# One layer of a hybrid decoder on one core: prompt attention moved between the products of the value stage

## The chip, the cores and the metric

The kernel runs on one NeuronCore of one Trainium2 chip. The metric is the device time of one execution in microseconds (us): the median over the timed runs. In the names below, PE is the matrix engine (TensorE), DVE the vector engine, ACT the scalar engine, POOL the general engine (GpSimd), which here also issues DMAs, and SP the queue that issues the weight loads.

## The reference, cut to what matters

One trunk layer handles a prompt of 272 tokens (16 meta tokens and 256 of the sequence) and 64 decode tokens (8 sequences of 8) with the same weights. What the change touches is the attention of the prompt and the state of the convolution:

```python
q = rmsnorm(q.reshape(B, T, N_HEADS, HEAD_DIM), q_g)      # 8 heads of 128
k = rmsnorm(k.reshape(B, T, N_HEADS, HEAD_DIM), k_g)
v = v.reshape(B, T, N_HEADS, HEAD_DIM)
...
s = index_scores(iqb, iwb, ik, qp, k_pos)                  # an indexer picks 64 keys per query
_, sel = lax.top_k(s, top_k)
logits = einsum('bqhd,bqkhd->bhqk', q, k_sel) * HEAD_DIM ** -0.5 + bias(rel)
p = softmax(logits); o = einsum('bhqk,bqkhd->bqhd', p, v_sel)
...
full = concatenate([ctx, u], axis=1)                       # 30 old rows of each sequence, then the new ones
```

The normed keys and the values of all tokens are outputs too (`k_prompt`, `v_prompt`, `k_sample`, `v_sample`), by token. The decode tokens attend to 64 pages of 128 cached keys; that work follows the prompt's attention.

## The kernel before, in words

All projections run with the output channels on the partitions and the 336 tokens as columns. A weight block of 2048 x 128 (one *unit*) is loaded to one of four slots of `RAW`; ACT rounds it to `WH`, DVE writes the rest to `WL`, four *quarters* each, two units ahead of PE; PE then multiplies it in 48 products (`split_mm`: `WH` with `XH`, `WH` with `XL`, `WL` with `XH`), 12 to a quarter, into one of two accumulators `psG`. The order of the work is written out by hand for each engine, and semaphores join the engines; nothing is scheduled. Each engine takes its own list strictly in order, PE too: a product that stands behind a wait waits with it.

Stages that matter here, in program order:

- **qk**: 16 units make queries and keys; DVE norms each (`nm_done` counts them) and takes the best scores of the indexer out in rounds of eight (`take8`). At its end DVE turns the scores of the prompt into a mask `Wp` (`p_mask`, before line 1060).
- **v**: 8 units, one for each head. ACT copies each accumulator to `vT`; PE turns it to token order (`v_by_token`, four turns), one unit later; DVE copies the turned tiles to `vtok`, `v2`, `vs` (`vk_done`).
- **prompt**: after the last value unit, 16 tiles (2 query tiles of 128 for 8 heads; the first sees 144 keys, the second 272). For tile i: PE makes logits (`p_logits`: query by key, and the mask added through the identity), DVE scales, adds the bias `Tb` and takes the maximum, ACT does the exponential (`p_soft`), DVE divides (`p_norm`), PE turns the weights (`p_turn`), ACT copies them to `pT`, PE multiplies them with the values (`p_values`), DVE copies the result to `oT`. The tiles go query tile by query tile, through four logit banks.
- **key turns**: 24 turns of the keys to token order through two banks; ACT copies them to `ktok`, which has two slots of two heads; heads 4 to 7 wait until the stores of heads 0 to 3 have landed (`ko_wr`). Then 128 small products give the logits of the decode tokens among themselves (`ln_mm`).
- **state turns**: 16 turns of the old convolution rows (`sct`), copied to `ub`.
- **cz**: 16 units of the convolution's input; between quarters PE turns one cached key page (8 turns) and after every second page multiplies it. POOL loads the pages into four slots of `kst`; it issues the first page after the last state turn has been copied (`sc_cp`), and page n + 4 when page n has been turned (`k_tr`).

Of the kernel before, what the change touches and what calls it, by code (L numbers as in the profile page):

```python
# [27 lines left out]
ALU = mybir.AluOpType  # L28
# [98 lines left out]
def place(persistent, transient):  # L127
# [42 lines left out]
    ("ub", [P, CT, UW], F32, ST_KOUT, ST_NORM),  # L170
    ("oT", [P, H, NQ], F32, ST_PROMPT, ST_WA),
# [31 lines left out]
    ("v2", [16, CC], F32, ST_V, ST_KOUT), ("Tb", [P, H, NP], F32, ST_V, ST_PROMPT),  # L203
    ("sct", [120, 2, CC], F32, ST_KOUT, ST_KOUT),
    ("Lp", [P, 4, NP], F32, ST_PROMPT, ST_PROMPT), ("pT", [P, 2, 3, P], F32, ST_PROMPT, ST_PROMPT),
    ("ktok", [P, 2, 3, 2 * P], F32, ST_KOUT, ST_KOUT), ("qsz", [P, H, B, 32], F32, ST_V, ST_CZ),

    ("kst", [P, 4, CC], F32, ST_CZ, ST_CZ), ("kTs", [P, 2, H, P], F32, ST_CZ, ST_CZ),
# [13 lines left out]
PLACING = ("Ss Ws SGA ub oT vs m8s cmp gsb QK qsz IW Sp Wp esel qm cms ikTa hT ML SGB L ikst oh iqT vtok iqs v2 iktok relb "  # L222
           "bT7 bNw relx vst CH CL Tb ikb osb wrow yp ya PTn ikT iwT rf cblk m8p xtok xs xTs kst OH csq rl sct kTs ktok "
           "ytok pairM Lp utok ustok pT sq rt vT sq2 gt at rp sel uss sgt crt sqa ut prow rln iwtok e8 ").split()


def layer(nc, I, O):
# [62 lines left out]
    with ExitStack() as ctx:  # L290
# [109 lines left out]
        def _(pool):  # L400
# [41 lines left out]

            pool.wait_ge(nm_done, 2 + 2 * H)
# [3 lines left out]
            pool.wait_ge(g_wr, 16)  # L447
            pool.dma_start(Tb[:], bass.AP(tensor=gscr, offset=P - 1, ap=[[RELW - 1, P], [P * RELW, H], [1, NP]])).then_inc(tb_ld, 16)
            pool.dma_start(O["conv_sample"][0, :, 0:CTX - Q], I["state_conv"][0, :, Q:CTX]).then_inc(cs_wr, 16)
            pool.wait_ge(vk_done, 2 + H)  # L450
            vp = O["v_prompt"][0, 0].rearrange("t h d -> t (h d)")
            pool.dma_start(vp[0:2 * P].rearrange("(i p) n -> p i n", p=P), vtok[:]).then_inc(v_wr, 16)
            pool.dma_start(vp[2 * P:NP], v2[:]).then_inc(v_wr, 16)
            pool.dma_start(O["v_sample"][0].rearrange("b q h d -> (b q) (h d)"), vs[:]).then_inc(v_wr, 16)
            pool.wait_ge(p_o, 2 * H)
            for i in range(2):
                pool.dma_start(sct[:, i, :], I["state_conv"][0, 4 * i:4 * i + 4].rearrange("b w c -> (b w) c")).then_inc(side_ld, 16)
            pool.memset(ub[:, :, 0:UPAD], 0.0).then_inc(ub_z, 1)
# [3 lines left out]
            for h in range(1, H, 2):  # L462
# [6 lines left out]
            pool.wait_ge(v_wr, 48)  # L469
            for i in range(4):  # L470
                pool.wait_ge(ko_wr[i], (16 if i < 2 else 32) * H // 4)
            pool.wait_ge(qs_dn, 1)
            pool.wait_ge(p_o, 2 * H)
            pool.wait_ge(sc_cp, CT)
# [9 lines left out]

            pool.sem_inc(k_tr, 4)
            k_pages = pages(kst, cache_k, k_ld, k_tr)
            k_pages(0)
            pool.dma_start(cblk[:], I["c_blk"]).then_inc(side_ld, 16)
# [44 lines left out]
        def _(act):  # L533
# [140 lines left out]
            def v(g):  # L674
                for s in range(4):
                    ahead(G0["v"] + g, s)
                    done(G0["v"] + g, s)
                    act.wait_ge(nm_done, 2 + 2 * H)
                    act.activation(vT[:, s % 2, :], G[s % 2][:, 0:NT], ACT.Copy).then_inc(ev[s % 2], 1)

            loop(act, GN["v"], v)

            act.wait_ge(qz, 1)
# [4 lines left out]
            def p_soft(i):  # L688
                nk = keys_of(i // H)
# [4 lines left out]
            p_soft(0)  # L694
            p_soft(1)
            for i in range(2 * H):
                if i + 2 < 2 * H:
                    p_soft(i + 2)
# [3 lines left out]
                full = i // H + 1  # L702
                act.activation(pT[:, i % 2, 0:full, :], MB[i % 2][:, 0:full * P].rearrange("p (k n) -> p k n", k=full), ACT.Copy)
                act.activation(pT[0:N_META, i % 2, full, :], MB[i % 2][0:N_META, full * P:full * P + P], ACT.Copy).then_inc(p_cp, 1)
            act.wait_ge(p_o, 2 * H)
            kp = O["k_prompt"][0, 0].rearrange("t h d -> t (h d)")
            for h in range(H):
# [5 lines left out]
                act.activation(ktok[:, slot, 0:2, c], TB[h % 2][:, 0:2 * P].rearrange("p (i d) -> p i d", i=2), ACT.Copy)  # L713
                act.activation(ktok[0:NT - 2 * P, slot, 2, c], TB[h % 2][0:NT - 2 * P, 2 * P:3 * P], ACT.Copy).then_inc(ko_cp, 1)
# [3 lines left out]
            for c in range(CT):  # L718
                act.wait_ge(sc_tr, c + 1)
                act.activation(ub[:, c, UP:UW].rearrange("p (b w) -> p b w", b=B)[:, :, 0:CTX],  # L720
                               MB[c % 2][:, 0:B * CTX].rearrange("p (b w) -> p b w", b=B), ACT.Copy).then_inc(sc_cp, 1)

# [3 lines left out]
            def cz(g):  # L726
                for s in range(4):
                    for j in range(4):
                        act.wait_ge(k_tr, g * 16 + (4 * s + j + 5))
                        act.activation(kTs[:, j % 2, 0:4, :], TB[0][:].rearrange("p (h n) -> p h n", h=4), ACT.Copy).then_inc(kc_A, 1)  # L730
                        ahead_quarter(G0["cz"] + g, s, j)
                    if s % 2 == 0:
                        done(G0["cz"] + g, s)
                        act.wait_ge(ev[1], 2 * (G0["cz"] + g) + (1 + s // 2))
                        act.activation(sgt[:], G[0][:, 0:NT], ACT.Sigmoid).then_inc(ev[0], 1)

            loop(act, GN["cz"], cz)
# [159 lines left out]
        def _(dve):  # L897
# [168 lines left out]
            def v(g):  # L1066
                def copy(s):
                    c = bass.ds(g * 4 * P + P * s, P)
                    dve.wait_ge(vtr, g * 4 + (s + 1))
                    dve.tensor_copy(vtok[:, :, c], MB[s % 2][:, 0:2 * P].rearrange("p (i d) -> p i d", i=2))  # L1070
                    dve.tensor_copy(v2[:, c], MB[s % 2][0:N_META, 2 * P:3 * P])
                    dve.tensor_copy(vs[:, c], MB[s % 2][0:NS, 3 * P:4 * P]).then_inc(vk_done, 1)

                ch.loop(g, 8)
                for s in range(4):
                    ahead(G0["v"] + g, s)
                    take8(m8s[:], Ws[:])
                    if s:
                        copy(s - 1)
                copy(3)  # L1080

            loop(dve, GN["v"], v)
            ch.end(GN["v"])


            sbank = [SB[0], SB[1], TB[0], TB[1]]

            def p_logits(i):
                qt, h = i // H, i % H
# [7 lines left out]
                dve.scalar_tensor_tensor(row, sbank[i % 4][:, 0:nk], SC, Tb[:, h, z0:z0 + nk], ALU.mult, ALU.add).then_inc(p_lg, 1)  # L1097
# [3 lines left out]
            def p_norm(i):  # L1101
                nk = keys_of(i // H)
# [5 lines left out]
            def p_out(i):  # L1108
                qt, h = i // H, i % H
# [3 lines left out]
            p_logits(0)  # L1113
            p_logits(1)
            for i in range(2 * H):
                if i + 2 < 2 * H:
                    p_logits(i + 2)
                if i >= 2:
                    p_out(i - 2)
                p_norm(i)  # L1120
# [4 lines left out]
            dve.wait_ge(ub_z, 1)  # L1125

            def cz(g):
                ch.loop(g, 8)
                for s in range(4):
# [13 lines left out]
                    done(G_, s)  # L1143
                    dve.tensor_tensor(ub[:, c, UPAD:UP], G[1][:, None, 0:NP], sgt[:, None, 0:NP], ALU.mult)
# [775 lines left out]
```

## Time and profile before

| | |
|---|---|
| median of 3 runs | 2144.13 us (2141.44 to 2153.07) |
| the profiled execution's own time | 2145.37 us |
| its span, first to last instruction | 2143.9 us |
| PE busy | 2064.7 us (96%) |
| DVE busy | 1247.2 us (58%) |
| ACT busy | 901.2 us (42%) |
| POOL busy | 165.7 us (8%) |
| mean granted clock of TensorE | 0.97 |

The page gives each engine's busy time over the whole span, and slices of it. The stretch that the change touches runs from 323.00 us, the first product of the value stage, to 457.37 us, the first turn of a cached key page. Rows of a timeline give the start in us, the time in us, the engine, the line, the operation and its operands, the count, and in brackets the idle time before it and what ended that. Weight products show a time longer than their pitch, since they are pipelined; a product of two fp32 operands shows as two records.

### The profile page before, as it was taken

The numbers are of one execution on the slowest core, as the hardware profiler recorded it, in microseconds if no ns is written. First come the engines' busy times: TensorE is split into PE (matmuls) and PEld (weight loads), VectorE is DVE, ScalarE is ACT, GpSimd is POOL, SyncE is SP. The second block draws the span as 40 slices with busy tenths as digits, with TensorE's granted clock in tenths as the row PEclk, the third lists the DMA queues.
The fourth block names the chain that finished last, engine by engine and source line by source line (L and its number), as shares of the span: only waits on it lengthen the run. The fifth ranks groups of instructions, "written<-read, shape, count | busy, mean of one in ns | idle before, by whom it ended". The sixth has DMA issues, their size and how long they took to land.

```text
span 2143.9 us, 40449 instructions
## 1 busy us (share of the span) xinstructions
PE 2064.7 (96%) x14517; PEld 1958.8 (91%) x14517; DVE 1247.2 (58%) x2293; ACT 901.2 (42%) x1647; POOL 165.7 (8%) x293
## 2 busy tenths in 40 slices
PE   6989999879998999999999999999999999999997
PEld 5956999769996777999999999999999999999997
DVE  5324988626666899875665545554455554445553
ACT  5423443434444333436444544543344443344443
POOL 6300000021112121001000000000000000000012
PEclk8997999879998999999999999999999999999999
DMA  8352456257776898455655555555555555555573
GB/s 232 93 113 40 122 133 172 66 163 237 239 240 197 267 327 271 133 143 155 191 156 148 146 156 139 155 147 147 157 143 151 153 142 156 149 145 157 144 207 110
DMA packets 545492, 350.54 MB, mean 164 GB/s; under 512 B 15122, under 2 KB 524346, under 8 KB 545007
## 3 DMA queue, kind: packets, MB, share of 16 engines
q1 hardware_dynamic: 518480, 263.55, 45.7%
q0 software_dynamic: 25824, 84.55, 12.4%
q8 instruction: 69, 1.13, 0.2%
q10 hardware_dynamic: 1088, 1.05, 0.1%
q14 instruction: 31, 0.25, 0.0%
HBM read 338.91 MB, written 10.83 MB: 163 GB/s over the span
## 4 chain that ended last, share of the span: by engine, by line
PE 67%; DVE 1%; ACT 0%; issue 0%; POOL 0%; POOLq 0%; DVEq 0%; ACTq 0%
PE psG L1380 21%; PE psG L1381 21%; PE psG L1382 20%; PE psS L1377 2%; PE psM L1380 1%; PE psM L1382 1%; PE psM L1381 1%; PE psM L1374 0%; PE psG L1374 0%; DVE stat L1186 0%; DVE OL L1249 0%; ACT L L752 0%; PE psT L1374 0%; DVE L L1181 0%; DVE L L1182 0%
## 5 line engine op out<-in xcount | busy, mean ns | idle before, releaser
L916 DVE TENSOR_TENSOR WL<-RAW,WH 128x512 fp32r<-128x512 f32 (+1 forms) x996 | 673.2, 691 | 642.9 <-ACT WH L551 641.3
L551 ACT ACTIVATE WH<-RAW 128x512 fp32r<-128x512 f32 (+1 forms) x996 | 615.7, 628 | 850.8 <-PE psG L1382 806.1
L1380 PE MATMUL psG<-XH,WH 128*128 128x320 f32 (+1 forms) x2688 | 854.5, 318 | 8.3 <-ACT iwT L629 5.3
L1381 PE MATMUL psG<-XL,WH 128*128 128x320 f32 (+1 forms) x2688 | 843.3, 314 | 0.0
L1382 PE MATMUL psG<-XH,WL 128*128 128x320 f32 (+1 forms) x2688 | 841.4, 313 | 0.0
L1380 PEld LDWEIGHTS psG<-XH,WH 128*128 128x128 f32 x2688 | 511.5, 190 | 40.1 <-issue 31.3
L1381 PEld LDWEIGHTS psG<-XL,WH 128*128 128x128 f32 x2688 | 511.8, 190 | 1.1
L1382 PEld LDWEIGHTS psG<-XH,WL 128*128 128x128 f32 x2688 | 511.8, 190 | 0.0
L1380 PE MATMUL psG<-MH,WH 128*128 128x320 f32 x960 | 297.9, 310 | 0.3 <-DVE ML L1349 0.3
L1382 PE MATMUL psG<-MH,WL 128*128 128x320 f32 x960 | 296.6, 309 | 0.0
L1381 PE MATMUL psG<-ML,WH 128*128 128x320 f32 x960 | 296.6, 309 | 0.0
L1380 PEld LDWEIGHTS psG<-MH,WH 128*128 128x128 f32 x960 | 180.5, 188 | 0.5 <-issue 0.5
L1381 PEld LDWEIGHTS psG<-ML,WH 128*128 128x128 f32 x960 | 180.5, 188 | 0.0
L1382 PEld LDWEIGHTS psG<-MH,WL 128*128 128x128 f32 x960 | 180.5, 188 | 0.0
L1213 DVE SCALAR_TENSOR_TENSOR ya<-ub,wdw,ya 128x256 f32<-128x256 f32 x232 | 99.8, 477 | 0.0
L522 POOL DMA_DIRECT2D out<-ytok x16 | 11.6, 726 | 1083.6 <-ACT ytok L876 1079.6
L1374 PE MATMUL psT<-ident,kst 128*128 128x128 f32 x512 | 68.9, 278 | 5.9 <-DMA kst<-in_cache_k 5.9
L1374 PEld LDWEIGHTS psT<-ident,kst 128*128 128x128 f32 x512 | 58.2, 142 | 12.8 <-issue 12.3
L1134 DVE COPY kTs<-psT 128x512 f32<-128x512 f32 x64 | 43.9, 686 | 42.8 <-PE psT L1374 42.8
L730 ACT ACTIVATE kTs<-psT 128x512 f32<-128x512 f32 x64 | 38.3, 598 | 46.5 <-PE psT L1374 46.2
L866 ACT ACTIVATE MH<-at 128x320 f32 x44 | 20.8, 472 | 82.9 <-DVE at L1347 82.9
L482 POOL DMA_DIRECT2D kst<-in_cache_k x64 | 33.8, 528 | 176.2 <-issue 176.2
(354 smaller groups left out, 1704.2 us busy)
## 6 DMA issues: line engine op xcount, KB each, us to landing
RAW<-in_w_in SPq DMA_DIRECT2D x160, 512.0 KB, 5.3
RAW<-in_w_ffn_down SPq DMA_DIRECT2D x96, 512.0 KB, 4.8
RAW<-in_w_ffn_gate SPq DMA_DIRECT2D x88, 512.0 KB, 4.9
RAW<-in_w_ffn_up SPq DMA_DIRECT2D x88, 512.0 KB, 4.6
kst<-in_cache_k POOLq DMA_DIRECT2D x64, 512.0 KB, 4.5
vst<-in_cache_v POOLq DMA_DIRECT2D x64, 512.0 KB, 5.9
RAW<-in_w_out SPq DMA_DIRECT2D x32, 512.0 KB, 4.8
RAW<-in_w_attn_br SPq DMA_DIRECT2D x16, 512.0 KB, 4.9
```

Of the source, the lines that this page charges most:

```text
L482: pool.dma_start(dst[:, n:n + 1, :], src[bass.ds(page(g * m + n, ptab2), 1)].rearrange("o s n -> s o n")).then_inc(landed[n], 16)
L551: act.activation(WH[:, s % 2, 4 * r:4 * r + 4, c], RAW[:, s, 4 * r:4 * r + 4, c], ACT.Copy).then_inc(hi_done, 1)
L730: act.activation(kTs[:, j % 2, 0:4, :], TB[0][:].rearrange("p (h n) -> p h n", h=4), ACT.Copy).then_inc(kc_A, 1)
L866: act.activation(MH[:, bass.ds(g * 2 + s // 2, 1), :], at2[:, s // 2:s // 2 + 1, :], ACT.Copy).then_inc(ah_dn, 1)
L916: dve.tensor_tensor(WL[:, s, k, c], RAW[:, s, k, c], WH[:, s % 2, k, c].bitcast(F32), ALU.subtract).then_inc(lo_done, 1)
L1134: dve.tensor_copy(kTs[:, j % 2, 4:8, :], TB[1][:].rearrange("p (h n) -> p h n", h=4)).then_inc(kc_D, 1)
L1213: ch.step(dve.scalar_tensor_tensor(z, x, tap, z, ALU.mult, ALU.add))
L1374: return pe.transpose(out, src, ident[0:n, 0:n])
L1377: return pe.matmul(out, lhsT, rhs, start=start, stop=stop, skip_group_check=True)
L1380: pe.matmul(out, WH[:, s % 2, k], hi, start=start, stop=False)
L1381: pe.matmul(out, WH[:, s % 2, k], lo, start=False, stop=False)
L1382: return pe.matmul(out, WL[:, s, k], hi, start=False, stop=stop)
```

## The change

The 16 tiles of the prompt's attention are now taken head by head (tile i is head i // 2, query tile i % 2) and placed behind the quarters of the value units: unit u carries the logits of head u, and the turns, the value products and the turns of the keys of head u - 1. The last head's rest follows behind the last unit. The value turns use bank `psT0`, the key turns bank `psT1`, the logits one bank for each query tile. The 16 state turns go to the first group of the cz stage, one pair behind each of its last eight quarters. POOL issues the bias table `Tb` earlier, and the first four key pages right after the last value copy (`vk_done`), ahead of the stores of the values; it waits for those stores, for the key stores and for `ln_mm` before it clears the padding of `ub` and goes on with page 4. Placement in SBUF (`PLACING` and the stages of some tiles) is changed to suit. The diff, cut to its core:

```diff
@@ POOL
+            pool.wait_ge(pp_acc, 2 * IH)
+            pool.wait_ge(d_ss, 1)
+            pool.wait_ge(g_wr, 16)
+            pool.dma_start(Tb[:], ...).then_inc(tb_ld, 16)
             pool.wait_ge(nm_done, 2 + 2 * H)
             pool.wait_ge(o_ik, 48)
             pool.memset(qsz[:], 0.0).then_inc(qz, 1)
...
-            pool.wait_ge(sc_cp, CT)
...
+            pool.wait_ge(vk_done, 2 + H)
             pool.sem_inc(k_tr, 4)
             k_pages = pages(kst, cache_k, k_ld, k_tr)
             k_pages(0)
+            pool.dma_start(vp[0:2 * P].rearrange("(i p) n -> p i n", p=P), vtok[:]).then_inc(v_wr, 16)
+            pool.dma_start(vp[2 * P:NP], v2[:]).then_inc(v_wr, 16)
+            pool.dma_start(O["v_sample"][0]..., vs[:]).then_inc(v_wr, 16)
+            keys_out(H - 1)
+            pool.wait_ge(p_o, 2 * H)
+            for i in range(2):
+                pool.dma_start(sct[:, i, :], ...).then_inc(side_ld, 16)
+            pool.wait_ge(qs_dn, 1)
+            pool.wait_ge(ln_mm, 1)
+            pool.wait_ge(v_wr, 48)
+            for i in range(4):
+                pool.wait_ge(ko_wr[i], (16 if i < 2 else 32) * H // 4)
+            pool.memset(ub[:, :, 0:UPAD], 0.0).then_inc(ub_z, 1)
             pool.dma_start(cblk[:], I["c_blk"]).then_inc(side_ld, 16)
             with pool.Fori(1, B * NPG // 4) as g:
                 k_pages(g)
@@ ACT
+            act.wait_ge(nm_done, 2 + 2 * H)
+            for u in range(H):
+                G_, s = G0["v"] + u // 4, u % 4
+                if u:
+                    v_kept(u - 1)
+                ahead_quarter(G_, s, 0)
+                if u:
+                    p_turned(2 * u - 2)
+                ahead_quarter(G_, s, 1)
+                if u:
+                    p_turned(2 * u - 1)
+                p_soft(2 * u)
+                ahead_quarter(G_, s, 2)
+                p_soft(2 * u + 1)
+                ahead_quarter(G_, s, 3)
+                if u:
+                    key_by_token(u - 1)
@@ DVE
+            for u in range(H):
+                G_, s = G0["v"] + u // 4, u % 4
+                if u:
+                    v_by_token(u - 1)
+                ahead_quarter(G_, s, 0)
+                best8(m8s[:], Ws[:])
+                p_logits(2 * u)
+                ahead_quarter(G_, s, 1)
+                taken8(m8s[:], Ws[:])
+                if u:
+                    p_out(2 * u - 2)
+                ahead_quarter(G_, s, 2)
+                p_logits(2 * u + 1)
+                p_norm(2 * u)
+                ahead_quarter(G_, s, 3)
+                if u:
+                    p_out(2 * u - 1)
+                p_norm(2 * u + 1)
@@ PE
+            for u in range(H):
+                G_, s = G0["v"] + u // 4, u % 4
+                x_quarter(G_, s, 0)
+                if u == 0:
+                    pe.wait_ge(nm_done, 2 + 2 * H)
+                    pe.wait_ge(p_mask, 2)
+                    pe.wait_ge(sqrt_done, 2 + 2 * H)
+                if u:
+                    v_by_token(u - 1)
+                    p_turn(2 * u - 2)
+                x_quarter(G_, s, 1)
+                if u:
+                    p_turn(2 * u - 1)
+                p_logits(2 * u)
+                x_quarter(G_, s, 2)
+                if u:
+                    p_values(2 * u - 2)
+                p_logits(2 * u + 1)
+                x_quarter(G_, s, 3)
+                if u:
+                    p_values(2 * u - 1)
+                    key_by_token(u - 1)
+            p_turn(2 * H - 2)
+            p_turn(2 * H - 1)
+            key_by_token(H - 1)
+            v_by_token(H - 1)
+            p_values(2 * H - 2)
+            p_values(2 * H - 1)
             pe.wait_ge(qs_dn, 1)
+            pe.wait_ge(p_o, 2 * H)
...
@@ PE, cz
                         x_quarter(G_, s, j)
+                        if g == 0 and s >= 2:
+                            state_turn(4 * (s - 2) + j)
```

PE's list of before at the end of the value stage (the turns of `vT`, then the first logits, the turn of the weights `Lp`, and the product of `pT` with the values) is this:

```order
L1374 MATMUL psM<-ident,vT 64x128
L1377 MATMUL psS<-QK 128x144
L1377 MATMUL psS<-Wp,ident 128x144
...
L1377 MATMUL psT<-QK 128x144
L1377 MATMUL psT<-Wp,ident 128x144
L1374 MATMUL psM<-ident,Lp 128x128
L1374 MATMUL psM<-ident,Lp 16x128
...
L1377 MATMUL psM<-pT,vtok 128x128 x2
```

In the list of now the same instructions stand inside a value unit, here the second one; each "..." is a quarter of 12 products into `psG`:

```order
L1392 MATMUL psT<-ident,vT 64x128
L1392 MATMUL psM<-ident,Lp 128x128
L1392 MATMUL psM<-ident,Lp 16x128
...
L1395 MATMUL psS<-QK 128x144
L1395 MATMUL psS<-Wp,ident 128x144
...
L1395 MATMUL psM<-pT,vtok 128x128 x2
L1395 MATMUL psS<-QK 128x272
L1395 MATMUL psS<-Wp,ident 128x272
...
L1395 MATMUL psM<-pT,v_120 128x128
L1392 MATMUL psT<-ident,QK 128x128 x2
L1392 MATMUL psT<-ident,QK 80x128
```

So a stretch of attention alone has become pieces between quarters of weight products, and the keys' turns (`psT<-ident,QK`) have moved there too.

POOL's list of before, from the stores of the values to the first key page (`kst`):

```order
L454 DMA out<-vs 64x1024
L457 DMA sct<-in_state_conv 120x1024 x2
L458 MEMSET ub 128x8x14
L465 DMA out<-ktok 16x256
L466 DMA out<-ktok 64x256
...
L418 TENSOR_LOAD ptab_62
L418 ISA x2
L482 ISA
L482 DMA kst<-in_cache_k 128x1024
```

And now, from the fourth key page to the loop that loads the others:

```order
L470 DMA kst<-in_cache_k 128x1024
L478 DMA out<-vtok 128x2x1024
L479 DMA out<-v_120 16x1024
L480 DMA out<-vs 64x1024
L458 DMA out<-ktok 16x256
L459 DMA out<-ktok 64x256
L484 DMA sct<-in_state_conv 120x1024 x2
L490 MEMSET ub 128x8x14
L491 DMA cblk<-in_c_blk 64x64
L492 UNCONDITIONAL_BRANCH
```

The first four pages have moved ahead of the stores of the values, and the stores, the state rows and the clearing of `ub` now stand between page 3 and page 4.

## Rows read from the trace of the kernel before

**Rows 1.** The page, part 1: PE's busy time, share and instructions.

```profile
PE 2064.7 (96%) x14517; PEld 1958.8 (91%) x14517; DVE 1247.2 (58%) x2293; ACT 901.2 (42%) x1647; POOL 165.7 (8%) x293
```

**Rows 2.** Stretches: start:end, length, busy PE, PEld, DVE, ACT, POOL; clock, DMA, GB/s.

```profile
323.00:385.20 62.20, 62.20 (x410) 61.88 (x409) 50.47 (x98) 22.81 (x40) 3.27 (x3) 1.00 0.60 165
385.20:432.44 47.24, 40.50 (x195) 31.50 (x192) 26.74 (x91) 19.45 (x75) 1.80 (x3) 0.80 0.18 52
432.44:448.10 15.66, 9.58 (x154) 7.56 (x153) 0.29 (x1) 4.22 (x16) 5.30 (x11) 0.51 0.50 152
...
457.37:461.62 4.25, 4.25 (x18) 4.25 (x18) 1.84 (x3) 0.60 (x1) 1.41 (x3) 0.50 0.94 339
...
472.54:479.17 6.63, 6.63 (x77) 6.21 (x73) 3.82 (x7) 3.83 (x6) 1.06 (x2) 1.00 0.97 304
```

**Rows 3.** Timeline of PE, first product of the value stage.

```profile
323.00 0.58 PE L1380 MATMUL psG<-XH,WH 128*128 128x336 f32 x1
```

**Rows 4.** Timeline of PE, value turns one unit apart.

```profile
338.09 0.60 PE L1374 MATMUL psM<-ident,vT 128*128 128x128 f32 x4
...
345.95 0.60 PE L1374 MATMUL psM<-ident,vT 128*128 128x128 f32 x4
```

**Rows 5.** Timeline of PE in the attention, at full clock.

```profile
410.49 0.38 PE L1374 MATMUL psM<-ident,Lp 128*128 128x128 f32 x2
410.70 0.80 PE L1377 MATMUL psM<-pT,vtok 128*128 128x128 f32 x4
411.43 0.73 PE L1377 MATMUL psT<-QK 128*128 128x272 f32 x2
...
415.81 0.73 PE L1377 MATMUL psS<-QK 128*128 128x272 f32 x2
...
416.83 0.49 PE L1374 MATMUL psM<-ident,Lp 128*128 128x128 f32 x3
417.16 0.61 PE L1377 MATMUL psM<-pT,vtok 128*128 128x128 f32 x4
...
418.12 0.50 PE L1377 MATMUL psT<-QK 128*128 128x272 f32 x1
```

**Rows 6.** Timeline of PE, the keys' turns held up and the logits behind them.

```profile
443.14 1.54 PE L1374 MATMUL psT<-ident,QK 128*128 128x128 f32 x6 [5.93 <-ACT ktok L714]
444.61 3.55 PE L1377 MATMUL psM<-QK,qsz 128*32 128x64 f32 x128
```

**Rows 7.** Timeline of all engines: last state copy, first page issues, first page turn.

```profile
451.22 0.64 ACT L720 ACTIVATE ub<-psM 128x240 f32<-128x240 f32 x2 [0.25 <-PE psM L1374]
...
453.65 0.55 POOL L482 DMA_DIRECT2D kst<-in_cache_k  x1 [7.11 <-issue]
454.84 0.53 POOL L482 DMA_DIRECT2D kst<-in_cache_k  x1 [0.64 <-issue]
...
457.37 0.87 PE L1374 MATMUL psT<-ident,kst 128*128 128x128 f32 x3 [5.93 <-DMA kst<-in_cache_k]
```

**Rows 8.** Timeline of DVE, the mask of the prompt.

```profile
330.46 1.71 DVE L1060 TENSOR_SCALAR Wp<-Wp 128x144 f32<-128x144 f32 x1
...
332.50 0.55 DVE L1060 TENSOR_SCALAR Wp<-Wp 128x272 f32<-128x272 f32 x1
```

**Rows 9.** Timeline of DVE, the copies of two heads' values.

```profile
389.16 0.41 DVE L1070 COPY vtok<-psM 128x256 f32 x1
...
389.88 0.40 DVE L1070 COPY vtok<-psM 128x256 f32 x1
```

**Rows 10.** DMA issues: count, KB each, median us from issue to landing.

```profile
kst<-in_cache_k POOLq DMA_DIRECT2D x64, 512.0 KB, 4.5
...
out<-vs POOLq DMA_DIRECT2D x1, 256.0 KB, 5.1
...
out<-iktok POOLq DMA_DIRECT2D x1, 16.0 KB, 33.7
```

More of the change, by code:

```diff
@@ L466, in _ @@
                 pool.dma_start(ks[:, c], ktok[NP - 2 * P:NT - 2 * P, slot, 2, :]).then_inc(ko_wr[2 + slot], 16)
[L469 to L473, printed above, removed]
-            pool.wait_ge(sc_cp, CT)
+            for h in range(1, H - 1, 2):
+                keys_out(h)
             def pages(dst, src, landed, used):
@@ L671, in _, with v_kept @@
             loop(act, GN["qk"], qk)
[L674 to L683, printed above, removed]
-            for h in range(H):
-                ins = act.activation(qsz[:, h, :, Q * (h % 4):Q * (h % 4) + Q], QK[:, h, NP:NT].rearrange("p (b q) -> p b q", b=B), ACT.Copy)
-            ins.then_inc(qs_dn, 1)
+            kp = O["k_prompt"][0, 0].rearrange("t h d -> t (h d)")
+            def v_kept(u):
+                done(G0["v"] + u // 4, u % 4)
+                act.activation(vT[:, u % 2, :], G[u % 2][:, 0:NT], ACT.Copy).then_inc(ev[u % 2], 1)
             def p_soft(i):
-                nk = keys_of(i // H)
+                nk = keys_of(i % 2)
                 act.wait_ge(p_max, i + 1)
@@ L692, in p_soft, with p_turned @@
                                accum_out=stat[:, 20 + i % 4:21 + i % 4]).then_inc(p_exp, 1)
[L694 to L698, printed above, removed]
+            def p_turned(i):
                 act.wait_ge(p_tr, i + 1)
@@ L717, in _, with state_turned @@
                     act.dma_start(kp[0:2 * P, P * (h - 1):P * (h + 1)].rearrange("(i p) n -> p i n", p=P), ktok[:, slot, 0:2, :]).then_inc(ko_wr[slot], 16)
-            for c in range(CT):
+            act.wait_ge(nm_done, 2 + 2 * H)
[15 more added lines that the diff above has]
+                    key_by_token(u - 1)
+            v_kept(H - 1)
+            p_turned(2 * H - 2)
+            p_turned(2 * H - 1)
+            key_by_token(H - 1)
+            act.wait_ge(qz, 1)
+            for h in range(H):
+                ins = act.activation(qsz[:, h, :, Q * (h % 4):Q * (h % 4) + Q], QK[:, h, NP:NT].rearrange("p (b q) -> p b q", b=B), ACT.Copy)
+            ins.then_inc(qs_dn, 1)
+            def state_turned(c):
                 act.wait_ge(sc_tr, c + 1)
+                act.wait_ge(ub_z, 1)
                 act.activation(ub[:, c, UP:UW].rearrange("p (b w) -> p b w", b=B)[:, :, 0:CTX],
@@ L1064, in _, with v_by_token @@
             dve.wait_ge(o_ik, 48)
[L1066 to L1086, printed above, removed]
+            def v_by_token(u):
+                c = slice(P * u, P * u + P)
+                dve.wait_ge(vtr, u + 1)
+                dve.tensor_copy(vtok[:, :, c], TB[0][:, 0:2 * P].rearrange("p (i d) -> p i d", i=2))
+                dve.tensor_copy(v2[:, c], TB[0][0:N_META, 2 * P:3 * P])
+                dve.tensor_copy(vs[:, c], TB[0][0:NS, 3 * P:4 * P]).then_inc(vk_done, 1)
             def p_logits(i):
-                qt, h = i // H, i % H
+                h, qt = i // 2, i % 2
                 nk, z0 = keys_of(qt), P * (1 - qt)
@@ L1108, in p_out @@
             def p_out(i):
-                qt, h = i // H, i % H
+                h, qt = i // 2, i % 2
                 dve.wait_ge(p_pv, i + 1)
                 dve.tensor_copy(oT[:, h, qt * P:qt * P + P], MB[i % 2][:, 3 * P:4 * P]).then_inc(p_o, 1)
[L1113 to L1120, printed above, removed]
+            for u in range(H):
[17 more added lines that the diff above has]
+            v_by_token(H - 1)
             p_out(2 * H - 2)
@@ L1124, in _ @@
             dve.sem_inc(kc_D, 1)
-            dve.wait_ge(ub_z, 1)
             def cz(g):
@@ L1614, in p_turn @@
             def p_turn(i):
-                full = i // H + 1
+                full = i % 2 + 1
                 pe.wait_ge(p_nrm, i + 1)
@@ L1658, in _, with state_turn @@
             ins.then_inc(ln_mm, 1)
-            pe.wait_ge(side_ld, 32)
-            pe.wait_ge(p_cp, 2 * H)
-            for c in range(CT):
+            pe.wait_ge(vk_done, 2 + H)
+            def state_turn(c):
+                if c == 0:
+                    pe.wait_ge(side_ld, 32)
                 if c >= 2:
```

110 lines of the change are left out of this document (47 added, 63 removed).

## The prediction

> **What bounds the kernel now.** I read the page's busy shares first. PE is busy for 2064.7 us of the span, DVE for little more than half of that [rows 1], so only PE's own list counts: work on another engine costs time only where PE waits for it. Next I cut PE's list into stretches [rows 2]. The value stage, 323.00 to 385.20, is 62.2 us without a gap, at full clock. The attention of the prompt, 385.20 to 432.44, is 47.24 us, with PE busy for 40.5 and a mean clock of 0.80. The keys' turns and the logits of the decode tokens take 15.66 us at 0.51. Then come the state turns and a wait for the first cached page, and the first products of the cz stage run at 0.50 for 4.25 us. The reader is to see that from 385.20 to 457.37 PE multiplies no weights at all, and that about half of the 72 us are waits or half clock. Last I read the places where PE waits: the keys' turns stand 5.93 us for a free slot [rows 6], the first page's turn 5.93 us for its landing [rows 7].
>
> The sum is made against the profiled execution (2145.37 us; its span of 2143.9 and 1.5 around it), which is 1.2 above the median of 2144.13. It compares two lengths between the same ends: first value product [rows 3] to first page turn [rows 7], 457.37 - 323.00 = 134.4 us before.
>
> **The units: 62.2 us, unchanged.** The eight units and seven of the eight value turns are the row of that stretch [rows 2]. Three turns of PE take 417.16 - 416.83 = 0.33 us at full clock [rows 5], 0.11 each. A unit's pitch is 345.95 - 338.09 = 7.86 [rows 4]; without its four turns (0.44) a quarter is 1.86.
>
> **The attention between the quarters: 30.4 us.** Logits of a long tile: 416.83 - 415.81 = 1.02; of a short one by its columns, 144 of 272: 0.54. Eight heads make 12.5. Turn and value products of a long tile: 418.12 - 416.83 = 1.29; of a short one 411.43 - 410.49 = 0.94 [rows 5]; seven heads (the eighth is in the tail) make 15.6. Three key turns a head, seven times 0.33, make 2.3. All of it lies on PE's path, since PE has no gaps there to put it in; what goes is not this work but the waiting around it.
>
> Whether PE waits for DVE and ACT inside a unit: the two stretches hold 77.2 us of DVE's work and, with the keys' copies, 46.5 of ACT's [rows 2], against 102.9 us of PE's path (62.2 + 30.4 + the 10.3 below), so neither is the bound. By order: from the logits of a long tile to its turn PE now has three quarters and the small pieces between, about 7.5 us, for a short one about 9. Before, 16 tiles passed in 47.24 us, 2.95 each, with about three in flight, so a tile's whole passage, half clock and queue included, was below 8.9. I take 0. Below nothing is excluded, since PE's work can't shrink; the upper bound is all that PE's attention lost before: 47.24 less eight times (1.56 + 2.23), 16.9 us.
>
> **The start of the value stage: 10.3 us added.** PE now waits behind the first quarter of unit 0 for `nm_done` and `p_mask`; before, it multiplied units 0 and 1 meanwhile, since the wait stood behind all eight units. The quarter ends at 323.00 + 1.86 = 324.9. DVE ends the mask at 332.50 + 0.55 = 333.05 [rows 8], and nothing of the change makes that earlier: the same norms and the same mask stand there, one of its steps at 1.71 us. So PE stands 8.2 us, and behind it wait units 0 and 1, whose weights are ready. The clock falls in such a gap: behind the idle 5.93 us at 457.37 [rows 7] PE ran at 0.50 for 4.25 us [rows 2], which costs half of that, 2.1. Bounds: 8.2 if the clock holds, 10.3 plus a second 2.1 if it returns as late again; I take 10.3, the row's own case.
>
> **The tail: 8.6 us.** After the last quarter stand two weight turns (0.55), three key turns, a value turn (0.44), 1.3 together; about 1 more, an estimate, for the last division on DVE, which stands behind that unit's last split. DVE copies the values of a head in 389.88 - 389.16 = 0.72 [rows 9]. From there POOL needs what it needed before between the last state copy's end (451.22 + 0.64) and its first page issue at 453.65, 1.8, and the page 457.37 - 453.65 = 3.7 to land [rows 7]: 8.5. PE's other arm is as long: value products (0.73 + 0.96), a copy, and the decode logits, 448.10 - 444.61 = 3.5 [rows 2, 6], make 8.7 with the 3.0 ahead of them. Bounds 7 (no late division, logits at full clock) to 11.
>
> So 62.2 + 30.4 + 10.3 + 8.6 = 111.5 stands against 134.4: 22.9 us less.
>
> **Given back in cz: 3.3 us.** The 16 state turns are now ordinary PE work between quarters, 16 x 0.11 = 1.8; ACT's copies lie beside the quarters, where ACT is busy for 3.83 of 6.63 us [rows 2]. And page 4 may come late. PE reaches it two page pairs after the first page turn, 2 x 6.63 = 13.3 us [rows 2]. POOL issues pages about 1.2 apart [rows 7], the fourth at about the moment of the first turn; then seven stores and state loads at 0.55 each, the last value store at about 1.8 behind that moment and the last key store at 2.9. It waits for their landing (5.1), clears, and issues page 4 at about 9.3, which lands 4.5 later [rows 10] at 13.8: 0.5 late. By volume (four pages, 1.3 MB of values, 0.3 of keys, 1.0 of state rows, 4.6 MB at the 339 GB/s of [rows 2]) the stores land at 10, page 4 at 16.4: 3.1 late. I take 1.5. Half clock at the start of cz was there before; I leave it.
>
> Net: 22.9 - 3.3 = 19.6 us off. 2145.4 - 19.6 = 2125.8 for a profiled run, 2124.5 against the median; I say 2125, with 2119 to 2131 as this case's own range.
>
> One row on the clock weighs against a worry about the turns: the pairs of pages at 472.54 to 479.17, with 16 turns among 24 products and 32 small ones, run at 1.00 [rows 2]. The Trainium skill, "TensorE: Matmul & The Clock Gate", section "Part 4: PE-mode transpose", says that transposes don't count as busy for the clock in the same way, so that they don't bring it up. By that rule alone the value units, thinned with turns, could run at half clock. By the row they don't, since those pages hold more turns to a product than the units will.
>
> **Rivals.**
> *The handoffs show.* DVE takes its list strictly in order: an early `p_logits` or `p_out` that waits for PE holds the split of the next quarter, ACT the same with `p_turned`. For it speaks that in the attention of before PE waited for just this passage; against it the 25 us that DVE has free. Up to 16.9 us come back: half of it gives 2133, all 2141. Chance 0.10.
> *More is won.* The clock holds over the start (2.1), page 4 is in time (1.5), the decode logits run at full clock and the first cz products too (up to 1.7 and 2.1): about 2118. The clock of 0.50 after each long gap before speaks against it. Chance 0.12.
> *POOL is held by a store, and the kernel is slower.* The wait before page 4 is on landings. A store of 16 KB queued behind a large write took 33.7 us to land [rows 10], and the value stores are now queued behind 2 MB of pages. Landing at 1.8 + 33.7, page 4 at 41.9, PE waits 28.6 instead of 1.5 and takes up at half clock (2.1): 2153.7. It is slower than before from a landing of about 24 us on. Against it: that write was of many small pieces, and the last store of the values landed in 5.1. Chance 0.04. A landing of about 12 us gives 2132; chance 0.07.
> *The turns count as idle.* If turns kept the clock down through the units, 62.2 + 30.4 us would double: about 2217. The row of the pages speaks against it. Chance 0.01.
>
> **How the numbers follow.** The forecast has 0.66. A measurement of this kernel can tell about 0.5% (10.7 us) from no change, so faster means below 2133.4: the forecast, the larger gain, half of the handoffs (0.05) and two thirds of the 12 us landing (0.05) make 0.88. Slower than 2154.9 are half of the held store and the idle turns, 0.03. The rest, 0.09, is the same. The range reaches from the larger gain with a little to spare, 2115, to half of the handoffs and the 12 us landing, 2136.
>
> **What would show it.** In the profile of the changed kernel: one idle stretch of PE of about 8 us behind the first quarter of the value stage, ended by DVE's mask (right for the start); unit pitches of about 11.6 us without idle time on PE and at clock 1.00 (the attention term; pitches of 13 or more mean the handoffs); the first page turn about 111 us after the first value product; in cz an idle PE for 0 to 3 us before page 4, ended by a DMA (longer: the store); products at 1.00 from a few us after the first gap. The forecast is wrong if the first page turn stands at the right place and the time doesn't follow, or if the units' pitch is far from 11.6.

## The result: 2124.65 us, 0.9908 of before

The changed kernel takes 2124.65 us (median of 5 runs, 2123.40 to 2129.68) against 2143.18 of the kernel before, run beside it (5 runs, 2141.44 to 2153.07). The ratio, worked out from all runs, is 0.9908, 95% interval [0.9883, 0.9934] (the quotient of the two medians is 0.9914): 18.5 us less, where 2125 was forecast. A second comparison (`r_after` below) gave 0.9920 [0.9892, 0.9947].

The page of the profiled execution (2124.80 us) begins as follows: its span, then busy time and share of the span of each engine. PE does as many instructions as before [rows 1] in 15.1 us less busy time, at a mean granted clock of 0.977 instead of 0.970. Of the 15.1 us, 3.9 lie ahead of the value stage.

```profile
span 2123.3 us, 40316 instructions
...
PE 2049.6 (97%) x14517; PEld 1948.1 (92%) x14517; DVE 1248.0 (59%) x2293; ACT 891.5 (42%) x1640; POOL 166.4 (8%) x293
```

The start of the value stage on PE's timeline: the first product, and the first one behind PE's wait (start, us, engine, line, tiles, shapes; in brackets the idle time ahead). Both answer to [rows 3].

```profile
318.81 0.57 PE L1398 MATMUL psG<-XH,WH 128*128 128x336 f32 x1
...
328.71 0.62 PE L1398 MATMUL psG<-XH,WH 128*128 128x336 f32 x1 [7.63 <-issue]
```

DVE's timeline shows what ended it, though the row says "issue": the last mask operation ends at 328.61, 0.1 us earlier. POOL's clearing of `qsz` stands beside the first. The kernel before had the same operations [rows 8].

```profile
326.28 1.70 DVE L1082 TENSOR_SCALAR Wp<-Wp 128x144 f32<-128x144 f32 x1
327.90 0.37 DVE L1081 TENSOR_TENSOR Wp<-Wp,Sp 128x272 f32<-128x272 f32 x1
328.31 0.30 DVE L1082 TENSOR_SCALAR Wp<-Wp 128x272 f32<-128x272 f32 x1
```

```profile
326.09 1.80 POOL L450 MEMSET qsz<- 128x2048 f32 x1 [124.18 <-DVE QK L1063]
```

Value turns on PE's timeline, two units apart in all, answer to [rows 4]: the pitch is 11.96 us now.

```profile
340.30 0.60 PE L1392 MATMUL psT<-ident,vT 128*128 128x128 f32 x4
...
352.26 0.60 PE L1392 MATMUL psT<-ident,vT 128*128 128x128 f32 x4
...
364.23 0.60 PE L1392 MATMUL psT<-ident,vT 128*128 128x128 f32 x4
```

Stretches (columns as in [rows 2]): behind the wait at the start; one whole value unit; the first unit of cz; the unit of page 4. In the value unit PE is busy without a gap at full clock, and DVE and ACT have 28% and 55% of their time free.

```profile
328.71:336.40 7.69, 7.69 (x33) 7.57 (x33) 4.07 (x9) 2.94 (x5) 0.00 (x0) 0.62 0.00 1
340.30:352.26 11.96, 11.96 (x81) 11.24 (x79) 8.61 (x23) 5.34 (x15) 0.00 (x0) 1.00 0.46 122
430.81:433.85 3.04, 2.92 (x20) 2.67 (x21) 1.84 (x3) 0.62 (x2) 2.47 (x5) 1.00 0.89 299
447.87:452.00 4.13, 4.13 (x21) 4.12 (x22) 1.84 (x3) 0.60 (x1) 0.53 (x1) 0.66 1.07 375
```

The end of the attention and cz on PE's timeline: the tail's waits, the decode logits, the first page's turn and page 4's; they answer to [rows 6, 7].

```profile
423.19 0.55 PE L1392 MATMUL psM<-ident,Lp 128*128 128x128 f32 x3 [0.56 <-DVE Lp L1113]
...
425.50 1.51 PE L1395 MATMUL psM<-pT,vtok 128*128 128x128 f32 x8 [0.99 <-DVE vs L1093]
...
427.90 1.99 PE L1395 MATMUL psM<-QK,qsz 128*32 128x64 f32 x128 [0.47 <-DVE oT L1118]
430.81 1.06 PE L1392 MATMUL psT<-ident,kst 128*128 128x128 f32 x8 [0.92 <-DMA kst<-in_cache_k]
...
447.87 1.97 PE L1392 MATMUL psT<-ident,kst 128*128 128x128 f32 x8 [3.47 <-DMA kst<-in_cache_k]
```

From first value product to first page turn PE takes 430.81 - 318.81 = 112.0 us, against 134.4: 22.4 off. From there to the end of cz (a product on `cblk` at 651.54; before at 673.25) it takes 220.7 against 215.9: 4.9 given back. That makes 17.5 us between the two ends. By the trace of `r_after` below it is 350.3 - 331.4 = 18.9, and the median's 18.5 lies between them.

The two profiled runs lie 20.6 apart, and the rest of that isn't the change's. The value stage of the run before began 4.2 us later. By 50 us it lay 2.8 us behind: the chip granted 0.66 of the clock there between 34 and 44 us and 1.00 in the changed kernel's run, with the same instructions. Another 1.3 us came between 72 and 83 us, at a clock of 0.53 against 0.70. Behind cz the changed kernel's run was 1.1 us longer; that part took 1470.6 to 1473.8 us in the ten profiles.

### The profile page after: what moved, and what is told of

It reads as the page before. It is cut to its first block, busy times and chain, and to the rows that moved or that the text cites. A ratio compares the mean times of both kernels' runs of the same rounds, so it can differ in the third digit from the quotient of the medians.

```text
span 2123.3 us, 40316 instructions
## 1 busy us (share of the span) xinstructions
PE 2049.6 (97%) x14517; PEld 1948.1 (92%) x14517; DVE 1248.0 (59%) x2293; ACT 891.5 (42%) x1640; POOL 166.4 (8%) x293
## 3 DMA queue, kind: packets, MB, share of 16 engines
q10 hardware_dynamic: 1088, 1.05, 0.2%
## 4 chain that ended last, share of the span: by engine, by line
PE 68%; DVE 1%; ACT 0%; issue 0%; POOL 0%; POOLq 0%; DVEq 0%; ACTq 0%
PE psG L1398 21%; PE psG L1399 21%; PE psG L1400 21%; PE psS L1395 2%; PE psM L1400 1%; PE psM L1399 1%; PE psM L1398 1%; PE psM L1392 0%; PE psG L1392 0%; DVE stat L1204 0%; PE psT L1392 0%; DVE OL L1267 0%; ACT L L774 0%; PE psS L1392 0%; DVE L L1199 0%
## 5 line engine op out<-in xcount | busy, mean ns | idle before, releaser
L525 POOL DMA_DIRECT2D out<-ytok x16 | 11.6, 728 | 1083.6 <-ACT ytok L898 1079.6
L1392 PEld LDWEIGHTS psT<-ident,kst 128*128 128x128 f32 x512 | 57.7, 142 | 11.6 <-issue 7.4
```

Of the source, the lines that this page charges most:

```text
L1392: return pe.transpose(out, src, ident[0:n, 0:n])
```

## Experiments

All kernels were run beside the kernel before. Its own runs there spread from 2134 to 2154 us, so a difference of 2 or 3 us between medians tells little by itself, and I give the traces' lengths beside them.

### e_state: the state turns alone

The kernel before, with the state turns in the first group of cz, the first pages issued without waiting for them, the padding cleared ahead of `cblk` and the placement of the changed kernel; the attention where it was. The diff shows PE's part of it.

```diff
-            for c in range(CT):
+            def state_turn(c):
...
                         x_quarter(G_, s, j)
+                        if g == 0 and s >= 2:
+                            state_turn(4 * (s - 2) + j)
```

> One half of the change alone, on the kernel before: the state turns in the first cz group, the first pages issued without waiting for them, the placement in SBUF of the changed kernel; the prompt's attention and the key turns stay where they were. Theory (in the kernel before the first page was held by the key stores' landing almost as long as by the state turns, so this half alone wins next to nothing): the first page turn comes about 2 us earlier, the 16 turns cost 1.8 in cz: 2143 us, ratio 1.000, within 2 us. Rival (the state turns and the page's landing behind them, 448.10 to 457.37, are free once moved): 9.3 us less 1.8, about 2136, ratio 0.9965.

Measured: 2141.30 us, ratio 0.9994 [0.9978, 1.001]. By the trace the first page turn comes 131.0 us after the first value product, 3.4 sooner, and cz then takes 217.5 instead of 215.9. About half of the step comes back, and the wait at the first page stays:

```profile
451.43 1.94 PE L1380 MATMUL psT<-ident,kst 128*128 128x128 f32 x8 [5.80 <-DMA kst<-in_cache_k]
```

So nearly all of the gain belongs to the other half: the attention and the key turns behind the units. The first pages ahead of the stores came with that half, and no run here parts the two.

### e_slack: more work for DVE

One more reduction of 128x1088 on DVE in each of the units 1 to 7; nothing reads it.

```diff
                 if u:
                     v_by_token(u - 1)
+                    dve.tensor_reduce(stat[:, 40 + u:41 + u], Tb[:, 0:4, :]..., AX, ALU.max)
```

> The changed kernel with one more DVE operation in each of the value units 1 to 7, a maximum over 128 x 1088 of the bias table, about 1.2 us, whose result nobody reads. Theory (PE is the bound in the units and DVE has about 3 us free in each): PE's unit pitch stays at 11.96 us and the time within 1.5 us of the changed kernel's 2124.65. Rival (the handoffs between PE, DVE and ACT are just met, or DVE's list sets the pitch): each unit grows by up to 1.2 us, 8 us in all, about 2133.

Measured: 2125.53 us, ratio 0.9918 [0.9895, 0.9941]. DVE's timeline has the 1.26 us, PE's has the value turns at the old pitch of 11.96, and no wait:

```profile
340.62 1.26 DVE L1124 TENSOR_REDUCE stat<-Tb 128x1 f32<-128x1088 f32 x1
...
352.58 1.26 DVE L1124 TENSOR_REDUCE stat<-Tb 128x1 f32<-128x1088 f32 x1
```

```profile
339.25 0.60 PE L1393 MATMUL psT<-ident,vT 128*128 128x128 f32 x4
...
351.21 0.60 PE L1393 MATMUL psT<-ident,vT 128*128 128x128 f32 x4
```

DVE's handoffs have at least this much room; no run loads ACT in the same way. The rival of the handoffs falls, by this run and by the units of the changed kernel. Page 4 is waited for longer in this profile than in the changed kernel's first one (3.47), with the same list on POOL:

```profile
448.75 1.97 PE L1393 MATMUL psT<-ident,kst 128*128 128x128 f32 x8 [5.67 <-DMA kst<-in_cache_k]
```

### e_memset: POOL's clearing behind the mask

```diff
             pool.wait_ge(o_ik, 48)
+            pool.wait_ge(p_mask, 2)
             pool.memset(qsz[:], 0.0).then_inc(qz, 1)
```

> POOL clears qsz after DVE's two mask rows and not beside them. In the changed kernel's trace the 144-column mask operation took 1.70 us and the 272-column one after it 0.30, while POOL's clearing of qsz (1.80 us) ran. Theory: DVE was slowed by POOL's writing; then the 144-column operation takes 0.2 to 0.3 us and PE's stall behind the first quarter falls from 7.63 to 6.2 us; the time falls by 1.4 us, less than one look can tell. Rival: the operation is long for a reason of its own (the first of its kind there); then it stays at 1.7 and the stall at 7.6 us.

Measured (a single run, 2125.01 us): DVE's mask operation takes 0.23 instead of 1.70 us, and PE's wait falls to 6.22.

```profile
324.51 0.23 DVE L1083 TENSOR_SCALAR Wp<-Wp 128x144 f32<-128x144 f32 x1
```

```profile
325.53 0.62 PE L1399 MATMUL psG<-XH,WH 128*128 128x336 f32 x1 [6.22 <-issue]
...
445.56 1.97 PE L1393 MATMUL psT<-ident,kst 128*128 128x128 f32 x8 [4.51 <-DMA kst<-in_cache_k]
```

The theory holds in size at the start. The first page turn comes 110.7 us after the first value product, 1.3 sooner, but PE then waits 4.51 us for page 4, and to the end of cz it takes 333.4 us against 332.7: in this profile nothing of it is left.

"Slowed" is the wrong word. In the changed kernel the DVE operation began at 326.28, POOL's clearing ended at 327.89, and DVE's operation at 327.98. In all eight profiles in which the two lie together, the kernel before among them, DVE's operation ends 0.08 or 0.09 us behind POOL's: it was held until POOL had done. The Trainium skill, "GPSIMD Engine Reference", section "8. Key points", says that GpSimd shares its SBUF interfaces with VectorE and contends with DVE in a 2-port mode or with two SBUF inputs. These rows have a contention of the two; which of the conditions held they don't show (the operation has one input in SBUF).

### e_start: the wait behind the fourth quarter

PE multiplies all four quarters of unit 0 before it waits for norms and mask; ACT's and DVE's lists of that unit follow suit.

```diff
-                x_quarter(G_, s, 0)
                 if u == 0:
+                    for r in range(4):
+                        x_quarter(G_, s, r)
                     pe.wait_ge(nm_done, 2 + 2 * H)
                     pe.wait_ge(p_mask, 2)
                     pe.wait_ge(sqrt_done, 2 + 2 * H)
+                    p_logits(0)
+                    p_logits(1)
+                    continue
+                x_quarter(G_, s, 0)
```

> The changed kernel with PE's wait for the norms and the mask, and the logits of head 0, behind the fourth quarter of value unit 0 instead of the first; ACT and DVE order their parts of head 0 to suit. Theory (the 7.6 us gap behind the first quarter is a pure wait for DVE's mask, and 2.9 us of half clock follow from it): the gap falls to about 2 us, because three more quarters (5.6 us) now run meanwhile, and the clock stays at 1.00: 8 us less, about 2116.5 us, ratio 0.9875. Rival (DVE's backlog sets the start, PE only waits elsewhere): the gap goes but PE waits as long in unit 1 or 2 for the splits or for the division, and the time stays within 2 us of the changed kernel's.

Measured: 2122.05 us, ratio 0.9899 [0.9875, 0.9924]; the profiled run 2119.34. At the start the theory holds. PE waits 2.08 us for the mask and 1.17 for a value copy instead of 7.63, and the clock stays at 1.00:

```profile
330.20 0.48 PE L1415 MATMUL psS<-QK 128*128 128x144 f32 x2 [2.08 <-issue]
...
334.87 0.66 PE L1412 MATMUL psT<-ident,vT 128*128 128x128 f32 x4 [1.17 <-ACT vT L681]
```

From first value product to that turn it is 334.87 - 320.29 = 14.58 us, 11.33 without the two waits. The changed kernel takes 340.30 - 318.81 = 21.49 for the same work, 13.86 without its wait: its half clock costs 2.53. So 6.9 us are won there. But at the end of the attention something new takes 3.02 us, in the middle of the 128 small products of the decode logits, and half clock follows:

```profile
422.56 1.88 PE L1415 MATMUL psM<-QK,qsz 128*32 128x64 f32 x118 [0.48 <-DVE oT L1126]
427.46 0.41 PE L1415 MATMUL psM<-QK,qsz 128*32 128x64 f32 x10 [3.02 <-issue]
427.83 1.53 PE L1412 MATMUL psT<-ident,kst 128*128 128x128 f32 x8
```

The first page turn comes after 107.5 us, 4.5 sooner than in the changed kernel. Page 4 isn't waited for then, and to the end of cz PE takes 325.8 us against 332.7: 6.9 less. The median moved by 2.6 only, where 8 was expected; the trace speaks for more of the gain than the median does. The rival's sign, a wait as long in unit 1 or 2, isn't there (1.17 us). What the wait among the small products is comes with the next kernel.

### r_after: the changed kernel again

> The changed kernel once more, on the chip of the three kernels beside it, so that they can be set against it there. If the gain is the kernel's and not the luck of one chip, its median is 2124.7 us give or take 2, and its ratio to the kernel before 0.991 give or take 0.002. If much of the 18.5 us was the phase of the clock in the stage of the indexer's queries (4.2 us of difference stood there between the two profiled runs), the ratio moves to 0.993 or beyond.

Measured: 2124.28 us (2117.79 to 2130.03), ratio 0.9920 [0.9892, 0.9947]. The gain is the kernel's. Its trace shows the wait among the small products too, in the very kernel whose first profile had none, and then no wait for page 4:

```profile
427.40 1.87 PE L1395 MATMUL psM<-QK,qsz 128*32 128x64 f32 x117 [0.48 <-DVE oT L1118]
432.30 0.41 PE L1395 MATMUL psM<-QK,qsz 128*32 128x64 f32 x11 [3.03 <-issue]
432.67 1.59 PE L1392 MATMUL psT<-ident,kst 128*128 128x128 f32 x8
...
447.47 1.09 PE L1392 MATMUL psT<-ident,kst 128*128 128x128 f32 x8
```

Now the first page turn takes 114.2 us from the first value product, and cz 217.2 from there: 331.4 in all, against 112.0 + 220.7 = 332.7. Page 4's turn stands 20.9 us behind the first page's issue in the first profile (447.87 - 426.97, with a wait of 3.47) and 21.0 in this one (447.47 - 426.49, without). PE loses 3 us or more and a stretch of half clock in one place or in the other. `e_start` has the wait among the small products too; set against this profile its first page turn comes 6.7 us sooner (107.5 against 114.2), so the gain at the start wasn't lost there.

The wait goes with an instruction fetch. The DMA queues of a stretch list it as `q8 instruction`. In the first profile it lies between 426 and 427, where the first page was just being issued; in this one between 429 and 430, 3 us behind that issue, among the page's packets:

```profile
q10 hardware_dynamic: 257, 0.25, 75.8%
q1 hardware_dynamic: 53, 0.02, 9.8%
q8 instruction: 1, 0.02, 6.6%
```

```profile
q0 software_dynamic: 63, 0.19, 81.1%
q8 instruction: 1, 0.02, 6.6%
```

In all eight profiles that have this change in the attention it is so: where the fetch lies within 1 us of the first page's issue, PE doesn't wait (the changed kernel, `e_pages`, `e_slack`, `e_memset`); where it lies 3 us or so behind, PE stands about 3 us at the 117th or 118th product (`r_after`, `e_start`, `e_stores`, `e_best`). What makes it late is open. The fetch's packet itself takes as long in either case (1.05 us in the first profile, 1.06 in this one). The page's packets may have kept it from starting, but in all four profiles with the wait it starts 0.5 to 0.7 us behind PE's stop, so it may as well have been asked for only then. No run here moved the one without the other.

### e_pages: pages 4 and 5 issued early

On the changed kernel: POOL issues pages 4 and 5 as their places come free, and waits for the landing of the stores and clears `ub` only then.

```diff
+            def ub_cleared():
                 pool.wait_ge(qs_dn, 1)
                 pool.wait_ge(ln_mm, 1)
                 pool.wait_ge(v_wr, 48)
...
-            with pool.Fori(1, B * NPG // 4) as g:
+            pages(kst, cache_k, k_ld, k_tr, {1: ub_cleared})(1)
+            with pool.Fori(2, B * NPG // 4) as g:
                 k_pages(g)
```

> The changed kernel with POOL issuing key pages 4 and 5 ahead of its wait for the stores and of the clearing of ub (pages 6 and 7 behind it). Theory (what the changed kernel gave back in cz is the late page 4): the 3.5 us of PE idle before page 4 and the 1.3 us of half clock behind it go, nothing else moves: 4.8 us less than the changed kernel, about 2120 us, ratio to before 0.989. Rival (the pages are late because the queue and the memory are full at that point: 2 MB of pages, 1.6 MB of stores, 1 MB of state rows): the wait only moves to page 4 or 6 with another releaser, and the time stays within 1 us of the changed kernel's.

Measured: 2121.71 us, ratio 0.9906 [0.9879, 0.9933]. Page 4 is issued 9.9 us behind the first page instead of 15.9, but takes 9.3 us from issue to landing, where the changed kernel's took 4.9:

```profile
434.25 0.56 POOL L470 DMA_DIRECT2D kst<-in_cache_k  x1 [1.16 <-issue]
```

```profile
kst<-in_cache_k POOLq DMA_DIRECT2D x1, 512.0 KB, 9.3
```

```profile
443.57 1.66 PE L1398 MATMUL psT<-ident,kst 128*128 128x128 f32 x8 [2.10 <-DMA kst<-in_cache_k]
```

PE's wait is 2.10 us, where the three profiles with the late issue and no wait among the small products have 3.47, 4.51 and 5.67 (the changed kernel, `e_memset`, `e_slack`). Half clock still follows (0.61 for 4.36 us), and cz takes 219.3 us instead of 220.7, 222.7 and 223.0. My theory, that POOL's wait for the stores costs the whole of it, falls: a wait of 2.10 is left, and the page's landing takes up most of the 6 us gained at its issue. The times don't decide between theory and rival: the median is 2.9 below the changed kernel's, the ratio nearly the same (0.9906 and 0.9908). Issued early, the page stands behind the stores and the state rows in POOL's list; whether the stores are what makes its landing long is what the next kernel asks.

### e_stores: the values' stores split

On `e_pages`: heads 0 to 6 are stored after head 6's copies, in the last unit.

```diff
+            pool.wait_ge(vk_done, 2 + H - 1)
+            values_out(slice(0, P * (H - 1)))
             pool.wait_ge(vk_done, 2 + H)
             pool.sem_inc(k_tr, 4)
...
+            values_out(slice(P * (H - 1), P * H))
```

> On top of the kernel that issues key pages 4 and 5 early: the stores of the values are split, and those of heads 0 to 6 (1.15 of 1.31 MB) leave in the last unit, where the DMA engines have nothing to do, and not behind the first four key pages. Theory: page 4 comes late there because it lies behind 1.3 MB of stores and 0.96 MB of state rows on the same DMA engines (9.1 us from issue to landing); with 1.15 MB gone PE's wait for page 4 falls from 2.10 to 0.5 us at most, the half clock behind it goes, and first page turn to end of cz falls from 219.3 to 217 us or below; median 2119, 2.5 below the kernel with early pages. Rival: the page waits for its own issue or for something the stores do not touch; then the wait stays at 2.1 us and the median at 2121.7.

Measured: 2117.96 us, ratio 0.9882 [0.9856, 0.9907]; 6.3 below `r_after` on the same chip. The early store of 896 KB landed in 4.1 us, the late one of 128 KB in 4.5, where the whole 1024 KB took 6.7 in the changed kernel:

```profile
out<-vtok POOLq DMA_DIRECT2D x1, 896.0 KB, 4.1
...
out<-vtok POOLq DMA_DIRECT2D x1, 128.0 KB, 4.5
```

PE doesn't wait for page 4 in the profile. It can't be credited to the edit alone, though, since this profile has the wait of 3.03 among the small products as well, and cz takes 217.2 us from the first page turn, as in `r_after` without the edit. Another row speaks against the theory: page 4 takes nearly as long from issue to landing as in `e_pages` (9.3), though 1.15 MB of stores no longer lie ahead of it.

```profile
kst<-in_cache_k POOLq DMA_DIRECT2D x1, 512.0 KB, 9.0
```

So those stores aren't what makes the landing long. The state rows and pages 1 to 3 still lie ahead of it; what holds it stays open. The median has the edit of `e_pages` in it as well, and its interval overlaps that of `r_after`: it speaks for the two edits together, and not strongly.

### e_best: all of it

`e_stores`, `e_start` and `e_memset` together, and head 7's values turned ahead of the last weight turn.

```diff
             p_turn(2 * H - 2)
+            v_by_token(H - 1)
             p_turn(2 * H - 1)
             key_by_token(H - 1)
-            v_by_token(H - 1)
```

> All of it: PE waits for norms and mask behind the fourth quarter of the first value unit, POOL clears qsz after the mask, head 7's values are turned ahead of the last probability turn, pages 4 and 5 are issued early, and the stores of heads 0 to 6 leave early. Theory, if the terms add: 7.4 (start) + 1.4 (clearing) + 1.0 (tail) + 4.8 (page 4 and the half clock behind it) = 14.6 us below the changed kernel, 2110 us, ratio 0.984. Rival: the attention's end is gated by something else, as in the kernel with the late start alone, where PE stood 3.0 us among the 128 small products before the first page turn; then 3 to 5 us of it come back there and the median is 2114 us or more.

Measured: 2110.47 us (2103.82 to 2117.18), ratio 0.9850 [0.9821, 0.9878], 13.8 below `r_after` (0.9920 [0.9892, 0.9947]); the sum said 14.6. That doesn't show each of its terms, since the one for page 4 wasn't borne out by the runs above. PE's wait at the start is down to 0.67 us and page 4 isn't waited for. The profiled run (2115.65) is one of the longer ones, and has the wait among the small products and half clock behind it:

```profile
328.20 0.48 PE L1429 MATMUL psS<-QK 128*128 128x144 f32 x2 [0.67 <-issue]
...
424.82 0.63 PE L1429 MATMUL psM<-QK,qsz 128*32 128x64 f32 x10 [2.90 <-issue]
425.39 1.97 PE L1426 MATMUL psT<-ident,kst 128*128 128x128 f32 x8
```

From first value product to the end of cz this run takes 323.9 us, against 332.7 and 331.4. The wait and the half clock behind it make about 5 us (2.90, and 8.17 us for the first two units at 0.50 and 0.93 instead of 5.89 in the changed kernel), which is what this run lies above the median. That the shorter runs are those without it is likely, but not shown: a run without profile has no rows.

## Why the prediction was right

The time (2125, measured 2124.65) and the mechanism were right. That the number came within 0.4 us is luck: the net of the sum was 19.6, and the traces have 17.5 and 18.9; the medians of the kernel before alone differ by 0.95 (2144.13 and 2143.18). The terms against the first profile:

- **Start of the value stage.** 10.3 forecast (8.2 and 2.1); measured 7.63 and 2.53. `e_start` shows the clock part directly, since without the long wait the same work ran at 1.00.
- **Units and attention between the quarters.** 62.2 + 30.4 = 92.6 forecast; 112.0 - 10.2 - 8.6 = 93.2 measured. The handoffs were taken at 0, and no wait stands in the units; that is the mechanism, and it held. The pitch of "about 11.6" that the text gave as its sign was an averaging slip: a unit of the middle has 7.86 + 1.56 + 2.23 + 0.33 = 11.98 by the prediction's own terms, and 11.96 was measured. The turns didn't hold the clock down: the row of the value unit has 1.00. The Trainium skill, "TensorE: Matmul & The Clock Gate", section "Part 4: PE-mode transpose", says that transposes don't count as busy for the clock in the same way; by that rule alone the units could have run at half clock, and here they didn't.
- **Tail.** 8.6 forecast; from the last unit's end (422.25) to the first page turn 8.56. Of the two arms, which the prediction held for equal, the page's ended it: the decode logits ran at full clock, 1.99 us instead of 3.55 [rows 6], so PE's arm was 0.92 shorter.
- **Given back in cz.** 3.3 forecast, 4.9 measured, and this is where the terms were off. State turns: 1.8 forecast; four pairs of pages with four turns each take 7.04 instead of 6.62, 1.7. Page 4: "I take 1.5" was mis-sized. It was a wait of 3.47, beyond the 3.1 of the bound by volume (4.51 and 5.67 in two other profiles), and 1.3 of half clock behind it that the term didn't have. POOL issued the page 12.1 us behind the first page turn (442.88), where the sum had 9.3. The stores landed in 6.2 to 7.2 us, not in 5.1 [rows 10], with four pages and 1 MB of state rows on the same engines. Against it stood "half clock at the start of cz was there before; I leave it": it went: PE comes there with a wait of 0.92 instead of 5.93, and the first unit takes 3.04 instead of 4.71 us at a clock of 1.00, 1.7 won. 1.7 + 3.5 + 1.3 - 1.7 = 4.8.
- **Not in the sum.** A fetch of PE's code that may come 3 us late at the end of the attention. It shows in four of the eight profiles. When it comes, PE reaches page 4 late enough to find it landed, so the length to the end of cz hardly changes (331.4 against 332.7).

The held store (2153.7) and the 12 us landing didn't come: the small store landed in 6.2 us.

## What to carry to other kernels

In this kernel, work with many short handoffs cost its own PE time and no more once it was laid between long products on the engine that bounds, with several of them from handoff to handoff; the gain is the waiting and the half clock that it had as a stage of its own. Price the two ends of such a stage by themselves, since the wait moved to its start (10.2 us) was the larger part of what could still be had. Where a load comes late, an earlier issue need not be an earlier landing: issued 6 us sooner, page 4 took 9.3 us to land instead of 4.9, and PE's wait fell from 3.47 to 2.10.

## What the runs showed that I had not expected

- One kernel has two patterns of waits with nearly one length: 3.03 us among 128 small products, or 3.47 us at page 4 (331.4 against 332.7 us). One profile alone would have named the wrong cause.
- A DVE operation of 0.23 us took 1.70 while POOL cleared 128x2048, and ended 0.09 us behind it, alike in eight profiles.
- A page's landing took 9.0 us with 1.15 MB of stores out of its way, and 9.3 with them ahead of it.
- The clock at the first products, 0.66 or 1.00 between 34 and 44 us with the same instructions, goes with 2.8 of the 4.2 us by which the start of the value stage differs.
